# One token tile's gates added into DRAM by index, and one top-k per head over all four token tiles, in a fused decoder block on one Trainium2 core

## The reference, cut to what matters

```python
q = (h @ w_q).reshape(B, T, PEER_HEADS, 2, PEER_HALF)      # 8 heads, 2 halves of 128
s = jnp.einsum('bthpd,hpnd->bthpn', q, sub_keys)           # 128 keys a half
v1, i1 = lax.top_k(s[..., 0, :], K)                        # K = 16
v2, i2 = lax.top_k(s[..., 1, :], K)
cand = (v1[..., :, None] + v2[..., None, :]).reshape(B, T, PEER_HEADS, K * K)
top_s, pos = lax.top_k(cand, K)
eidx = ...                                                 # i1 * 128 + i2 at pos
gates = jax.nn.softmax(top_s, axis=-1)
u = jnp.take(u_tab, eidx, axis=0)                          # 16384 experts
act = jax.nn.gelu(jnp.einsum('btd,bted->bte', h, u))
vv = jnp.take(v_tab, eidx, axis=0)
out = jnp.einsum('bte,bted->btd', gates * act, vv)
```

## Time and profile before

| | |
|---|---|
| time, median of 3 runs | 1856.96 us (1856.75 to 1858.47) |
| span of the profiled execution, first to last instruction | 1856.8 us |
| TensorE busy | 1768.2 us, 95% |
| VectorE busy | 1307.3 us, 70% |
| GpSimd busy | 764.5 us, 41% |
| ScalarE busy | 742.8 us, 40% |
| mean granted TensorE clock | 0.981 of full speed |

### The profile page before, as it was taken

One profiled execution on the slowest core, in us unless ns is written; L12 is line 12 of the kernel. 1 busy time (PEld: TensorE's weight loads), 2 busy tenths in 40 slices (PEclk: granted clock), 3 DMA queues, 4 the chain that ended last, 5 costly groups with the idle time before them and its releaser, 6 DMA issues. The chain is left out here.

```text
span 1856.8 us, 31058 instructions
## 1 busy us (share of the span) xinstructions
PE 1768.2 (95%) x11485; PEld 1564.7 (84%) x11485; DVE 1307.3 (70%) x2777; ACT 742.8 (40%) x1227; POOL 764.5 (41%) x449
## 2 busy tenths in 40 slices
PE   3999999999998989999999999879999999999998
PEld 2666888878877889999999999879998888888887
DVE  5993454553224679878869999756787888777777
ACT  4332332242234233333337767633333333333334
POOL 2333232344442448777753333122454443332330
PEclk9998999999999999999999999989999999999999
DMA  9661101022322249888868999978899999889883
GB/s 356 217 233 71 36 16 34 25 91 91 102 79 103 91 141 314 282 292 292 286 235 281 341 311 331 319 264 285 287 317 337 370 370 359 326 320 328 316 325 145
DMA packets 179267, 432.64 MB, mean 233 GB/s; under 512 B 15816, under 2 KB 91720, under 8 KB 179040
## 3 DMA queue, kind: packets, MB, share of 16 engines
q1 hardware_dynamic: 125088, 273.71, 42.5%
q0 software_dynamic: 36864, 134.23, 20.3%
q10 hardware_dynamic: 17216, 23.36, 3.4%
HBM read 383.54 MB, written 47.71 MB: 232 GB/s over the span
## 5 line engine op out<-in xcount | busy, mean ns | idle before, releaser
L201 POOL DMA_INDIRECT own_rows<-in_peer_v_dram,own_row x128 | 212.3, 1659 | 330.8 <-DVE y_own L2094 312.7
L1988 PE MATMUL banks<-v_hi,coef_lo 128*128 128x512 f32 x756 | 294.6, 390 | 0.0
L1988 PE MATMUL banks<-v_lo,coef_hi 128*128 128x512 f32 x756 | 294.5, 390 | 0.0
L1988 PE MATMUL banks<-v_hi,coef_hi 128*128 128x512 f32 x756 | 294.1, 389 | 0.1
L201 POOL DMA_INDIRECT own_rows<-in_u_rows_dram,own_row x128 | 160.6, 1255 | 233.1 <-DVE own_rows L1733 178.8
L2079 DVE TENSOR_TENSOR v_lo<-weight_ring,v_hi 128x1024 fp32r<-128x1024 f32 x128 | 156.5, 1222 | 24.7 <-ACT v_hi L2027 22.7
L1988 PEld LDWEIGHTS banks<-v_hi,coef_hi 128*128 128x128 f32 x756 | 142.0, 188 | 29.5 <-issue 0.5
L1988 PEld LDWEIGHTS banks<-v_hi,coef_lo 128*128 128x128 f32 x756 | 141.9, 188 | 29.5
L1988 PEld LDWEIGHTS banks<-v_lo,coef_hi 128*128 128x128 f32 x756 | 141.9, 188 | 28.9
L2094 DVE SCALAR_TENSOR_TENSOR y_own<-own_rows,own_coef,y_own 128x1024 f32<-128x1024 f32 x128 | 163.8, 1279 | 1.9 <-DVE y_own L2094 0.5
L1397 PE MATMUL banks<-h_hi,wring_hi 128*128 128x384 f32 (+2 forms) x448 | 155.2, 347 | 4.0 <-ACT gelu_early L1479 2.9
(11 more groups left out here) (393 smaller groups left out, 4346.1 us busy)
## 6 DMA issues: line engine op xcount, KB each, us to landing
weight_ring<-in_peer_v_dram SPq DMA_DIRECT2D x128, 512.0 KB, 5.4
weight_ring<-in_peer_u_dram SPq DMA_DIRECT2D x68, 512.0 KB, 4.5
ada<-in_w_ada_dram SPq DMA_DIRECT2D x48, 512.0 KB, 5.7
gate_scratch<-gate_block SPq DMA_DIRECT2D x48, 512.0 KB, 7.0
gate_tiles<-gate_scratch SPq DMA_DIRECT2D x32, 768.0 KB, 6.9
gelu_scratch<-gelu_early ACTq DMA_DIRECT2D x104, 192.0 KB
gelu<-gelu_scratch SPq DMA_DIRECT2D x104, 192.0 KB, 5.6
u_early<-in_peer_u_dram SPq DMA_DIRECT2D x36, 512.0 KB, 7.1
```

What stands on the lines that cost most here:

```text
L201: pool.indirect_dma_start(own_rows[:, n % R], None, tables[n // NS], bass.IndirectOffsetOnAxis(ap=own_row[:, n % NS:n % NS + 1], axis=0)). ...
L1988: last = nc.tensor.matmul(y_bank(t, half)[:], w[:, j, t * P:(t + 1) * P], x[:, j, c], start=(first and n == 0), stop=False)
```

## The change

The third dense tile (NSC = 1) is still multiplied with every expert, but its gates no longer pass through one-hot matrices: VectorE works out an address for each of its gates, and GpSimd adds the 128 x 1 gates of one rank to the table in DRAM by an indirect DMA with an add, 16 of them a head (`add_gates`). SP writes zeros over that part of the table in the delta stage (8 DMAs of 1 MB). The scatter loop so has 4 turns instead of 6.

There is one top-k per head over all four tiles. The order of pieces is new: 4 query tiles and 2 u tiles, then for each head 10 or 11 u tiles with the two query tiles for the head after next among them, then 2 u tiles: 104 pieces, so 20 more u tiles are done in the retrieve stage (12 come from the scatter stage, 8 from the expert stage). VectorE now makes the lo part of three pieces in four, GpSimd of the fourth (`by_pool`). The softmax is done per head: the exponential on ScalarE after the first u tile of the next head, the rest (`weigh`) at `fill(h, 4)`. Dots: none in head 0, 9 in heads 1 to 6, 10 in head 7, 8 in each turn of the scatter loop, 160 rows instead of 144 in the expert stage.

```diff
-U_HEAD, U_MID, U_TAIL, U_UNITS = 8, 2, 2, (0, 1, 2, 4, 5, 6)
+NSC = 1
+NHOT = TD - NSC * P
+U_HEADS, U_MID, U_TAIL, U_UNITS = (10,) * 4 + (11,) * 4, 2, 2, (0, 1, 2, 4, 5, 6)
-NR = TD // (2 * TB)
+NR = NHOT // (2 * TB)
-DOT_HEAD, DOT_ITER = 8, 8
+DOT_HEADS, DOT_ITER = (0,) + (9,) * 6 + (10,), 8
+POOL_LO = True
-OWN_GELU = 8
+OWN_GELU = 12
+def pieces():
+    out = [("q", n) for n in range(4)] + [("u", n) for n in range(U_MID)]
+    u = U_MID
+    for h, n in enumerate(U_HEADS):
+        for m in range(n):
+            out.append(("u", u))
+            u += 1
+            if m in (2, 4) and 2 * h + 4 < 2 * PH:
+                out.append(("q", 2 * h + 4 + (m == 4)))
+    return out + [("u", u + n) for n in range(U_TAIL)]
...
-    return 0 if j == 0 else 1 if j < 3 else 1 + (i < 14)
+    return 2 if p % 11 == 0 else 1
...
+                def add_gates(pool, h, n):
+                    if n == 0:
+                        if h:
+                            pool.wait_ge(gates_added, 16 * NSC * TOPK * h)
+                        else:
+                            pool.wait_ge(gates_zeroed, 16 * ZERO_PARTS * NSC)
+                    t, k = n // TOPK, n % TOPK
+                    pool.indirect_dma_start(gates_at, bass.IndirectOffsetOnAxis(ap=add_at[:, h, t, k:k + 1], axis=0),
+                                            gates[:, h, HOT_TILES + t, k:k + 1], None, compute_op=ALU.add).then_inc(gates_added, 16)
...
+        DVE_FROM = B0 + HR
+        FILLS = 17
+        def by_pool(n):
+            return n < DVE_FROM or POOL_LO and (n < FIRST[1] + HR and n % 2 == 0 or n % 4 == 2)
+        def pieces_of(h):
+            return range(max(FIRST[h] + HR, DVE_FROM), min(FIRST[h + 1] + HR, NPIECE) if h < PH - 1 else NPIECE)
...
             @block.gpsimd
-                for n in range(HR - 1, B0 + HR):
-                    rest(n)
-                pool.wait_ge(*VO.after("own_row"))
...
+                for n in (*range(HR - 1, DVE_FROM), *pieces_of(0)):
+                    if by_pool(n):
+                        rest(n)
+                at = 0
+                for h in range(1, PH):
+                    before = sum(DOT_HEADS[:h])
+                    pool.wait_ge(*V.after("own_row", h - 1))
+                    todo = pieces_of(h)
+                    for j in range(TOPK):
+                        for n in todo[j * len(todo) // TOPK:(j + 1) * len(todo) // TOPK]:
+                            if by_pool(n):
+                                rest(n)
+                        while at < before + R + DOT_HEADS[h] * (j + 1) // TOPK:
+                            fetch(pool, at)
+                            at += 1
+                        if j == 0:
+                            pool.wait_ge(*VG.after("gate", h - 1))
+                        for n in range(j * NSC, (j + 1) * NSC):
+                            add_gates(pool, h - 1, n)
...
+                def fill(h, i):
+                    todo = pieces_of(h)
+                    for n in todo[i * len(todo) // FILLS:(i + 1) * len(todo) // FILLS]:
+                        if not by_pool(n):
+                            rest(n)
+                    for n in range(i * DOT_HEADS[h] // FILLS, (i + 1) * DOT_HEADS[h] // FILLS):
+                        dot(sum(DOT_HEADS[:h]) + n)
+                    if i == 4 and h:
+                        weigh(h - 1)
```

More of the change, by code:

```diff
@@ L1332, in retrieve_stage @@
     NB = N_PROJ + 4 * KT
-    B0 = NQ + U_MID
-    T0 = B0 + PH * U_HEAD
-    NPIECE = T0 + U_TAIL
+    ORDER = pieces()
+    NPIECE = len(ORDER)
+    B0 = 4 + U_MID
+    FIRST = [ORDER.index(("u", U_MID + sum(U_HEADS[:h]))) for h in range(PH)] + [NPIECE - U_TAIL]
+    DVE_FROM = B0 + HR
+    FILLS = 17
+    SC = slice(HOT_TILES, ND)
     with ExitStack() as ctx:
@@ L1462, in _, with turn_lists @@
-                early(T0 + U_TAIL - 1)
+                def turn_lists():
+                    for n in range(3):
+                        pe.wait_ge(*(V.after("sel1", PH - 1) if n < 2 else VP.after("hot_gate")))
+                        for t in range(HOT_TILES):
+                            src = sel[:, n, t].rearrange("p h k -> p (h k)") if n < 2 else hot_gate[:, t]
+                            last = nc.tensor.transpose(bank[2 + n][:, t * P:(t + 1) * P], src, C["ident"])
+                        last.then_inc(turned, 1)
@@ new lines, in _ @@
+                for n in range(2):
+                    product(n)
+                for k in range(KT):
+                    for n, x in enumerate((h_hi, h_lo)):
+                        last = nc.tensor.matmul(bank[6 + k // 4][:, k % 4 * P:(k % 4 + 1) * P], x[:, k, TD:T].bitcast(F32), C["ident"],
+                                                start=(n == 0), stop=(n == 1))
+                last.then_inc(h_turned, 1)
+                for n in range(2, B0):
+                    product(n)
+                    if n == 2:
+                        scores(0)
@@ L1464, in _ @@
+                for h in range(PH):
+                    for n in range(FIRST[h], FIRST[h + 1]):
+                        product(n)
+                        if n == FIRST[h + 1] - 4 and h + 1 < PH:
+                            scores(h + 1)
+                for n in range(FIRST[PH], NPIECE):
+                    if n == NPIECE - 1:
+                        turn_lists()
+                    product(n)
             @block.scalar
@@ L1617, in topk @@
+                    fill(h, 14)
                     by_rank = lambda x: x.rearrange("p t (k r) -> p t k r", r=TOPK)
@@ L1649, in _ @@
[L1649 to L1654 removed]
+                        nc.vector.tensor_reduce(sel[:, n, :, h, :], by_rank(hot[:, n]), AX.X, ALU.add).then_inc(*V.step(f"sel{n}"))
@@ L1888, in _ @@
                 body(0, True, first=True)
-                with sp.Fori(1, NR - 1) as i:
+                for i in range(1, NR - 1):
                     body(i, True)
```

437 lines of the change are left out of this document (198 added, 239 removed).

## The result

The changed kernel takes 1906.3 us (median of 4 runs, 1904.97 to 1909.61), the kernel before, on the same chip, 1856.86 (1855.99 to 1858.47). The ratio is 1.0267, 95% interval 1.0253 to 1.0282: 2.7% slower, 26 us above the forecast of 1880.4 and inside its range.

The account below looks back on a forecast made before the run. The prediction took TensorE's list of work as the bound: 1819.5 us without new waits, plus 43.4 of waits and 17.5 of slow clock, gave 1880.4 us. Its range was 1836 to 1915, its main case 1866 to 1898.

Parts of the forecast that it names:

- the price of what stands ahead of GpSimd's first lo part: GpSimd's queue in heads 2 and 3, behind the gate: add 1.25, gather 1.1, add 1.25, lo part 2.5, 6.1 us.
- My ceiling: Upper case of the forecast: adds at 1.66 us, about 9 us more waits, slow clock at all eight: 1897.5 us.
- all eight waits: TensorE waiting in each head from 1 to 7, and for the gates at the end: 43.4 us together.
- The sign I gave: In the profile after, GpSimd's adds taking over 1.7 us would show that the forecast is low.
- the moment that the prediction calls A: In a head of the retrieve stage, when TensorE is done with piece FIRST + 2; gate put at 3.3 us later.
- The base: Whole kernel without new waits: 1856.8 less 28.8 for removed scatter units and 8.5 for old waits and clock, 1819.5 us.
- The clock: TensorE's slow clock behind seven of the eight new waits, 2.5 us each: 17.5 us.
- The two sides of SBUF: VectorE's lo parts, with two SBUF inputs, waiting for GpSimd's lo parts: about 5 us, left out of the sum.
- The floor: Rival: TensorE's waits at the heads are short, 29 us, and the clock gives back early: 1850 to 1866, chance 0.15.
- TensorE without waits: Rival: TensorE doesn't wait at the heads, only the removed units count: 1819.5, up to 1845 us, chance 0.21.
- Dear adds: Rival: an add by index takes GpSimd 2.5 us, waits come to about 84 us: 1925 us, chance 0.12.
- The DMA engines as the bound: Rival: the DMA engines become the bound of the expert stage, 6 us on top: 1886 us, chance 0.05.

Follow-up runs that it names:

- e5: The changed kernel with its 128 adds by index into the table made plain writes by index: 1892.99 us.
- e10: Changed kernel with every lo part on VectorE, dots 10 in heads 1 to 5 and 7 in heads 6 and 7, gates normalised at fill 1: 1828.96 us.
- e3: The changed kernel with all lo parts from piece 9 on made by VectorE, GpSimd only gathering and adding: 1838.82 us.
- e8: Changed kernel without the adds, all three dense tiles through one-hot matrices, six scatter turns, 9 u tiles a head, all lo parts on VectorE: 1868.69 us.
- e1: The changed kernel with GpSimd's wait for the gate and its adds moved from j = 0..15 to j = 3..15, behind the first lo part: 1844.05 us.
- e2: The changed kernel without its 128 adds by index, GpSimd still waiting for the gate at the same place: 1858.52 us.
- e6: The changed kernel with every lo part on VectorE, and 10 dots in heads 1 to 5 and 7 in heads 6 and 7: 1836.27 us.
- e4: The changed kernel with the last head's gates normalised at fill 1 instead of fill 4: 1870.53 us.

## Why the prediction was off: point by point

**The step that failed** is the price of what stands ahead of GpSimd's first lo part: "An add by index isn't in the trace. It writes 128 descriptors as a gather does ... I take 1.25." That sentence holds for a write by index (e5: 1.08 long, 0.30 to the next) and not for an add: 1.56 at the least, 1.67 in the mean, 0.30 to the next, some of 2.4. My ceiling, 1.66, was the mean; I chose by the wrong neighbour. The mechanism was right, and so was the place of all eight waits; their size, 43.4 us, was not, and a ninth place, behind the later pieces of head 7, was missing. The ceiling would not have saved the sum: its waits are 52.4 us, since 1.66 was counted there from one start to the next, where the adds take 1.87, and its "about 9 us" more don't follow from its own numbers (0.41 us for each of 15 adds are 6.2). The sign I gave, an add over 1.7 us, isn't met by a mean of 1.67 either: it is a length, and my 1.25 was a distance. TensorE's waits by head, in us:

| | forecast | e5, writes | after, adds |
|---|---|---|---|
| head 1 | 6.4 | 5.76 | 7.66 |
| head 2 | 4.0 | 4.29 | 6.33 |
| head 3 | 4.0 | 4.28 | 6.33 |
| head 4 | 6.2 | 7.02 | 7.66 |
| head 5 | 9.2 | 9.37 | 9.94 |
| head 6 | 1.7 | 5.79 | 8.68 |
| head 7, first | 8.4 | 9.35 | 11.14 |
| head 7, later pieces | 0 | 0 | 5.36 |
| the gates at the end | 3.5 | 3.14 | 3.13 |
| sum | 43.4 | 49.0 | 66.2 |

Of the 22.8 us too few, 17.2 are the adding (last column less the one before) and 5.6 are in the forecast even with writes. Of the 17.2, the 15 adds that stand ahead of the pieces of the prediction are 8.9 at 0.59 us each (an estimate: 1.67 - 1.08), the later pieces of head 7 are 5.4, and the rest is gates that come later and operations held up at other places (below). 4.1 of the 5.6 are head 6, the one wait sized wrongly by itself. VectorE ends the normalising of that head's gates thus in the changed kernel:

```profile
1006.57 0.22 DVE L1599 TENSOR_TENSOR gates<-gates,gate_sum 128x64 f32<-128x64 f32 x1
```

TensorE runs dry at 1022.01 - 8.68 = 1013.33, and three u tiles of 4.18 earlier, at 1000.8, was the moment that the prediction calls A. The gate comes at A + 6.0 (in e5 at A + 5.1, and the first write starts at A + 5.8). I had put it at A + 3.3, as in heads 2 and 3, although I had called VectorE level with TensorE in heads 6 and 7: 2.5 of the 4.1. Most of the other 1.6 is two long ones among the five writes of e5, 1.91 and 1.35 us. The "later pieces" of head 7, which I left out, are adds alone: e5 doesn't have them.

**The base was right.** 1819.5 us without new waits. e10 has the same list of work and 3.40 + 3.70 us of waits: 1827.5 - 7.1 = 1820.4. The agreement is a little better than earned: 1819.5 still holds the 1.69 us that TensorE waits at the first unit of the scatter stage before, and 1820.4 some 3 us of slow clock behind the two waits (0.77 over 5.8 us, 0.76 over 7). The units removed: 28.8 forecast, 29.9 between e3 and e8. The moved u tiles, dots, gathered rows, zeros and the exponential cost nothing that shows here.

**The clock: right in size, by another count.** Forecast 17.5 us. The retrieve stage of the changed kernel is 555.7 us, 488.0 without its waits (66.2, and 1.5 at the scatter stage's first unit); that of e10 is 1049.92 - 573.70 = 476.2, less 7.1 = 469.1. The slow clock is 18.9 us, more than in e10, which has a slow stretch of its own. Counted over the 7 us behind each wait, by granted clocks from 0.60 to 0.78, it is 19.4 us at nine waits, 2.2 each: I had taken seven waits of 2.5. The ninth is the wait for the gates, 3.13 us, with 0.76 behind it. That the two sums agree is luck in part: two stretches too few, and each a little too long. From e10's 1820.4, 1820.4 + 66.2 + 18.9 + 1.5 = 1907.0 us, 0.9 over the span.

**VectorE was no bound in heads 1 to 5**, as forecast: e3 gives it all lo parts and TensorE's first wait comes in head 7.

**The two sides of SBUF were on the path, by another door.** I had priced VectorE's lo parts waiting for GpSimd's, at 5 us, and left it out. They hardly wait: of 68 in the retrieve stage, 63 take 1.2 us, as in e10, where GpSimd makes none, and the other five 1.4, 1.4, 1.5, 2.5 and 4.2. What waits is the add. The lo part of VectorE that runs while the add of 741.87 above starts, and the same pair in head 7:

```profile
741.63 1.23 DVE L1584 TENSOR_TENSOR wring_lo<-weight_ring,wring_hi 128x1024 fp32r<-128x1024 f32 x1 [2.87 <-ACT wring_hi L1510]
...
1065.33 1.20 DVE L1584 TENSOR_TENSOR wring_lo<-weight_ring,wring_hi 128x1024 fp32r<-128x1024 f32 x1
...
1065.36 2.60 POOL L246 DMA_INDIRECT gate_scratch<-gates,add_at  x1 [6.53 <-DVE top_half L1619]
```

The first add is 2.43 us long, 0.87 more than 1.56, and the lo part had 0.99 to run when it started; the second is 1.04 longer, with 1.17 to run. It holds throughout the stage: 17 adds start inside a lo part of VectorE's, and 16 of them are longer than 1.56 by what was left of it less 0.10 to 0.14 us (the other had 0.15 left); of the 95 that start outside one, none is over 1.71. The writes of e5 (19 of 19) and, but for one of 1.92 us in e10, the adds of e1, e3 and e10 do the same. Ahead of the pieces that TensorE waits for there are four such adds, in heads 2, 3, 6 and 7, 3.1 us together, and one such gather in head 1, 0.9. So about 4 of the 66.2 us of waits come from this, in a place where I had put nothing; it is read from the times alone, no run tests it. The Trainium skill, "SBUF — State Buffer", section "SBUF: two separate sides", which has a VectorE operation with two SBUF inputs and a GpSimd operation that reads SBUF lock each other out, is borne out in kind: by VectorE's lo part of 4.22 us at 1086.06, beside one of GpSimd's, and by the adds, which take their addresses from SBUF.

**The rivals.** The floor (waits of 29 us) fell: they are 66.2, and even e2, without any add, has 27.6. TensorE without waits fell for this kernel, but it is what e3, e6 and e10 are, one line away, and its time, 1819.5 up to 1845, is theirs. Dear adds: nearest to the truth, at 1.87 us from start to start, instead of the 2.5 that I priced. Its 84 us of waits have no working beside them: 15 adds at 1.25 more are 19 us, which makes 62. The DMA engines as the bound: refuted, share 0.99 at 374 GB/s and no wait.

## What to carry to other kernels

Before work is put on an engine that is idle half of the time, list what stands behind it in that engine's order: here the wait for a gate, two adds and a gather stood ahead of the one lo part that TensorE needed next, and a loss of 49 us became a gain of 18 when those products went to another engine (e3), 28 with two small moves more (e10). Where an operation has no row in the trace, take its ends for the sum of everything that waits behind it, and look at what it does beyond its nearest neighbour (here it adds, and its nearest neighbour doesn't) before choosing the cheap end. Say of each price whether it is a length or the distance from one start to the next. When a wait is moved, look for the second condition behind it (e4: the landing of the adds before), which decides what the move is worth.

## What the runs showed of the hardware

- An indirect DMA of 128 x 4 bytes into DRAM costs GpSimd 1.08 us as a write and 1.67 as an add. The next one starts 0.30 us behind its end in either case. The difference is on the issuing engine and not only in the transfer. Which part of the descriptor work makes it isn't settled.
- A tensor operation on GpSimd that follows such an add is recorded from 0.55 us before the add's record ends, and so reads 2.93 us instead of 2.38. Lengths of the two are not to be summed; ends are.
- An indirect DMA that GpSimd starts while VectorE subtracts 128 x 1024 from 128 x 1024, both in SBUF, is longer by the rest of the subtraction less about 0.12 us (16 adds of the changed kernel, up to 2.60 us instead of 1.56). The subtraction isn't: e3 and e10 have 95 of them each in the retrieve stage, beside adds and gathers, none over 1.3 us. GpSimd's own subtraction does hold VectorE's up: 4.11 us for one that starts at 744.76 in e5, beside GpSimd's from 745.41 to 747.77.
- How long TensorE was idle doesn't alone say whether the clock falls. Behind a wait of 2.16 us the granted clock over 7 us is 0.76 in e1 (1009.31) and 1.00 in e4 (851.60); behind one of 1.79 us in e3 it is 0.76, and behind one of 3.13 us in e1 (1059.55) 1.00.
- The clock can fall after the wait and not with it. In e1 the wait of 3.88 us at 988.70 is followed by three matmuls at the high level (starts 0.17 to 0.25 us apart) and then by 0.33 us from start to start, and 0.76 over the 7 us. The first matmul behind a wait therefore doesn't tell what the wait costs.
